# Hybrid decoder step on one core: outer products of the sample states in four row groups of the array, head norms copied to four quadrants

## What is computed

```python
# both head groups: the state is decayed by a number and gets a rank-one update
S = S * exp(g)  + outer(k, beta * (v - exp(g) * S.T @ k))     # delta rule, 128x128
C = C * f       + i * outer(k, v)                             # mLSTM, 128x128
# per head of 128 features, q and k before the recurrence and all outputs after it
q = q * rsqrt(sum(q*q) + eps) * 128**-0.5
k = k * rsqrt(sum(k*k) + eps)
o = o * rsqrt(mean(o*o) + eps) * w * gate
h = concat(o_A, o_B) @ w_out                                  # 264 x 1024 by 1024 x 1024
x = LayerNorm(alpha * x + h)
```

## Time and profile before

| | before |
|---|---|
| median of 3 runs | 1038.25 us (1035.95 to 1038.7) |
| profiled execution, its own time | 1048.3 us |
| its span | 1046.6 us |
| TensorE busy, share of span | 929.4 us, 89% |
| VectorE busy | 408.8 us, 39% |
| ScalarE busy | 175.7 us, 17% |
| GpSimd busy | 226.0 us, 22% |
| mean granted clock of TensorE | 0.931 |

### The profile page before, as it was taken

The page is one execution under the profiler, slowest core; times in us unless marked ns, Lnnn a source line. Parts: engine busy times, 40 slices in busy tenths (PEclk is TensorE's granted clock), DMA queues, the critical chain, the costliest instruction groups (busy, mean ns, idle before and its releaser), DMA issues.

```text
span 1046.6 us, 12023 instructions
## 1 busy us (share of the span) xinstructions
PE 929.4 (89%) x4804; PEld 506.3 (48%) x4804; DVE 408.8 (39%) x829; ACT 175.7 (17%) x309; POOL 226.0 (22%) x334
## 2 busy tenths in 40 slices
PE   6999988998993799999989768989938999999993
PEld 4888867985342333333323366844414333333330
DVE  3799318634546121222224165912272111111115
ACT  0411221223001111111101242211111111110111
POOL 4579962301312511001100200000012111100000
PEclk9999986997996799999999978979977999999997
DMA  9446639002639589999999915561097789999982
GB/s 261 99 167 249 238 128 312 1 11 93 221 116 394 215 309 407 405 404 399 414 398 427 418 46 160 177 268 46 3 404 294 277 364 409 407 402 404 416 358 83
DMA packets 83578, 277.51 MB, mean 265 GB/s; under 512 B 25337, under 2 KB 44231, under 8 KB 60854
## 3 DMA queue, kind: packets, MB, share of 16 engines
q1 hardware_dynamic: 70298, 255.86, 63.8%
q10 hardware_dynamic: 10660, 16.49, 4.9%
q0 software_dynamic: 2560, 4.33, 1.4%
HBM read 261.49 MB, written 18.01 MB: 267 GB/s over the span
## 4 chain that ended last, share of the span: by engine, by line
PE 73%; DMA 16%; DVE 6%; ACT 2%; issue 1%; ACTq 1%; POOL 0%; SPq 0%; DVEq 0%; POOLq 0%
PE ps L1756 17%; DMA ring<-in_moe_w_up 13%; PE ps L320 11%; PE ps L1780 7%; PE ps L2427 6%; PE ps L1798 3%; PE ps L761 3%; PE ps L1735 3%; PE ps L2304 2%; PE ps L736 1%; DMA work<-in_ln_ffn_b 1%; PE ps L609 1%; PE ps L2274 1%; PE ps L1434 1%; PE ps L1486 1%
## 5 line engine op out<-in xcount | busy, mean ns | idle before, releaser
L1756 PE MATMUL ps<-ring,work 128*64 128x512 f32 x480 | 217.3, 604 | 10.0 <-DMA ring<-in_moe_w_up 8.5
L1757 PE MATMUL ps<-ring,work 128*64 128x512 f32 x480 | 217.4, 604 | 0.0
L1756 PEld LDWEIGHTS ps<-ring,work 128*64 128x64 f32 x480 | 63.6, 138 | 136.5 <-issue 120.6
L1840 DVE TENSOR_TENSOR work<-ps,work 64x512 f32<-64x512 f32 x32 | 33.8, 1056 | 221.7 <-ACT work L1811 221.7
L320 PE MATMUL ps<-work,ring 128*128 128x264 f32 x512 | 115.2, 387 | 0.0
L1780 PE MATMUL ps<-ring,work 128*64 128x512 f32 x248 | 113.0, 598 | 2.3 <-DVE work L1845 1.4
L1781 PE MATMUL ps<-ring,work 128*64 128x512 f32 x248 | 113.1, 598 | 0.0
L320 PEld LDWEIGHTS ps<-work,ring 128*128 128x128 f32 x512 | 96.8, 190 | 16.4
L1202 POOL TENSOR_TENSOR ring<-ring 128x512 f32<-128x512 f32 (+5 forms) x76 | 90.5, 1208 | 9.0 <-DVE ring L1198 5.7
L1850 DVE COPY work<-ps 64x512 f32<-64x512 f32 x32 | 22.2, 694 | 150.7 <-PE ps L1781 150.7
L1861 POOL COPY work<-work 64x1 int32<-64x1 int32 x32 | 5.7, 178 | 336.2 <-PE ps L1735 298.2
(11 more groups left out here) (496 smaller groups left out, 1248.3 us busy)
## 6 DMA issues: line engine op xcount, KB each, us to landing
ring<-in_moe_w_down SPq DMA_DIRECT2D x31, 2048.0 KB, 16.0
ring<-in_moe_w_gate SPq DMA_DIRECT2D x60, 1024.0 KB, 14.6
ring<-in_moe_w_up SPq DMA_DIRECT2D x60, 1024.0 KB, 16.8
ring<-in_w_in ACTq DMA_DIRECT2D x6, 2048.0 KB, 8.5
s_out_mats<-ring SPq DMA_DIRECT2D x4, 1280.0 KB, 4.7
ring<-in_w_in SPq DMA_DIRECT2D x2, 2048.0 KB, 10.3
s_in_mats<-ring SPq DMA_DIRECT2D x4, 1024.0 KB, 6.3
ring<-in_w_out SPq DMA_DIRECT2D x1, 4096.0 KB, 17.1
```

Of the source, the lines that this page charges most:

```text
L1756: nc.tensor.matmul(ps[0:SLOT, 5, :], xgT[s][:, c], gate_w[slot][:, c], start=c == 0, stop=c == DC - 1)
L1757: last = nc.tensor.matmul(ps[SLOT:P, 5, :], xgT[s][:, c], up_w[slot][:, c], start=c == 0, stop=c == DC - 1)
L1840: nc.vector.tensor_tensor(hid[s][0:SLOT].rearrange("t (c p) -> t p c", c=4), strided(ps[SLOT:P, 5, :]), strided(sg[s][SLOT:P]), ALU.mult). ...
```

## The change

1. The 0/1 operands that pick a head are now one 64-column row `head_row` with a one in column 31; `head_col(h, n)` is a slice of n columns of it with the one in column h.
2. Both sums of squares are computed four times, once for each quadrant of 32 output partitions (four 32-column matmuls for one 8-column matmul), so that `R` has the 8 head rows in each quadrant. ln and exp run over all 128 partitions. The spreading matmul of head h contracts over the 32 rows of quadrant h % 4.
3. The turning of keys and values to rows is done four times too, by matmuls with the identity instead of one transpose, so `krow` has its 32 rows in each quadrant (`rows_by_quadrant`; the VectorE copies cover 128 partitions).
4. The 16 masked operands become 4: 128 rows by 512, where quadrant r of batch b is the old operand 4b + r (`pair_mask`, eight small VectorE copies at the start, holds the mask).
5. An outer-product batch is four matmuls with 32-row contraction, in the four row groups, into four banks, with one step at the end.
6. The batches stand elsewhere: batch 0 where groups 0 to 2 stood; batch 1 after the spreading matmuls; batches 2 and 3 after k-steps 2 and 6 of tile 0. Batches 2 and 3 use banks 2 and 3 as well, so tile 1 now waits for update 15. VectorE does updates 0 to 3 before the multiplies, 4 to 15 after `merged`.

```diff
-        head_col = view(const, C0["heads"], 8, 8)
+        head_row = view(const, C0["heads"], 64)
+        pair_mask = const[:, C0["cols"] + 8:C0["cols"] + 16].rearrange("p (b c) -> p b c", c=4)
+        def quad(r):
+            return slice(32 * r, 32 * r + 32)
+        def quad_row_of(r, h):
+            return ident[quad(r), 32 * r + h:32 * r + h + 1].to_broadcast([32, P])
+        def head_col(h, n):
+            return head_row[:, 31 - h:31 - h + n]
...
+            for r in range(4):
+                for b in range(2):
+                    nc.vector.tensor_copy(pair_mask[quad(r), b], ident[quad(r), 36 * r + 16 * b:36 * r + 16 * b + 4]).then_inc(*dv.done("pair_mask"))
...
             for h in range(8):
-                last = nc.tensor.matmul(ps[0:8, 0, 0:T], head_col[:, h], sq[:, h], start=h == 0, stop=h == 7)
+                for r in range(4):
+                    last = nc.tensor.matmul(ps[quad(r), 0, 0:T], head_col(h, 32), sq[:, h], start=h == 0, stop=h == 7)
             last.then_inc(*pe.done("ss"))
...
-                nc.tensor.matmul(ps[:, h, 0:T], row_of(h, 8), R[0:8, RA], start=True, stop=True).then_inc(*pe.done(f"rn{h}"))
+                nc.tensor.matmul(ps[:, h, 0:T], quad_row_of(h % 4, h), R[quad(h % 4), RA], start=True, stop=True).then_inc(*pe.done(f"rn{h}"))
...
+        def rows_by_quadrant(dst, columns):
+            for r in range(4):
+                last = nc.tensor.matmul(dst[quad(r)], columns, ident, start=True, stop=True)
+            return last
...
-            nc.tensor.transpose(ps[0:HS, 3, P:2 * P], kq[:, 0], ident).then_inc(*pe.done("krow"))
+            rows_by_quadrant(ps[:, 3, P:2 * P], kq[:, 0]).then_inc(*pe.done("krow"))
...
-        def pe_outer(t, g):
-            t.wait_ge(*po.at(f"vblk{g}"))
-            if g < 3:
+        OUTER_BANK = (4, 5, 6, 7, 4, 5, 6, 7, 2, 3, 4, 5, 6, 7, 2, 3)
+        def pe_outer(t, b):
+            t.wait_ge(*po.at(f"vblk{b}"))
+            if b == 0:
                 t.wait_ge(*dv.at("hB"))
                 t.wait_ge(*ac.at("oA"))
+                t.wait_ge(*dv.at("s_final"))
             else:
-                t.wait_ge(*dv.at(f"new{g - 3}"))
-            nc.tensor.matmul(banks(5 + g % 3), krow[0:HS, 0 if g < 8 else 2], flat(vblk[g % 2][0:HS]), start=True, stop=True).then_inc(*pe.done(f"outer{g}"))
+                t.wait_ge(*dv.at(f"new{(0, 3, 5, 9)[b]}"))
+            if b == 2:
+                t.wait_ge(*dv.at("norm_o7"))
+            for r in range(4):
+                last = nc.tensor.matmul(banks(OUTER_BANK[4 * b + r]), krow[quad(r), 0 if b < 2 else 2], flat(vblk[b % 2][quad(r)]),
+                                        start=True, stop=True)
+            last.then_inc(*pe.done(f"outer{b}"))
...
             for i in range(TT):
+                if i == 1:
+                    t.wait_ge(*dv.at("new15"))
                 residual_pe(t, i, 2 * i)
...
-                    if i == 0 and k < 7:
-                        for g in range(3 + 2 * k, min(5 + 2 * k, 16)):
-                            pe_outer(t, g)
+                    if i == 0 and k in (2, 6):
+                        pe_outer(t, 2 + k // 6)
...
-            nc.scalar.activation(R[0:8, RA], ps[0:8, 0, 0:T], ACT.Ln, bias=eps_rms[0:8], scale=1.0 / DK).then_inc(*ac.done())
+            nc.scalar.activation(R[:, RA], ps[:, 0, 0:T], ACT.Ln, bias=eps_rms, scale=1.0 / DK).then_inc(*ac.done())
...
-            for g in range(16):
+            for b in range(4):
...
+                nc.gpsimd.tensor_tensor(vblk[b % 2], krow[:, 1 if b < 2 else 3].unsqueeze(1).to_broadcast([P, 4, P]),
+                                        pair_mask[:, b % 2].unsqueeze(2).to_broadcast([P, 4, P]), ALU.mult).then_inc(*po.done(f"vblk{b}"))
```

More of the change, by code:

```diff
@@ L582, in mix_pe @@
             t.wait_ge(*dv.at("krow0"))
-            nc.tensor.transpose(ps[0:HS, 3, 2 * P:3 * P], small[:, 3], ident).then_inc(*pe.done("vrow"))
+            rows_by_quadrant(ps[:, 3, 2 * P:3 * P], small[:, 3]).then_inc(*pe.done("vrow"))
             ml_pe_rden(t)
@@ L685, in ml_pe_state @@
                 for i in range(TT):
-                    last = nc.tensor.matmul(ps[0:H, 7, 0:P], head_col[:, h, 0:H], kwk[:, 4 * i + h], start=(h, i) == (0, 0),
+                    last = nc.tensor.matmul(ps[0:H, 7, 0:P], head_col(h, H), kwk[:, 4 * i + h], start=(h, i) == (0, 0),
                                             stop=(h, i) == (H - 1, TT - 1))
@@ L705, in ml_pe_den @@
                 den = ps[0:H, 6, 0:SEQ]
-                nc.tensor.matmul(den, head_col[:, h, 0:H], wexp[:, h, 0:SEQ], start=h == 0, stop=False)
-                last = nc.tensor.matmul(den[:, P:SEQ], head_col[:, h, 0:H], wexp[:, h, SEQ:384], start=False, stop=h == H - 1)
+                nc.tensor.matmul(den, head_col(h, H), wexp[:, h, 0:SEQ], start=h == 0, stop=False)
+                last = nc.tensor.matmul(den[:, P:SEQ], head_col(h, H), wexp[:, h, SEQ:384], start=False, stop=h == H - 1)
             last.then_inc(*pe.done("den"))
@@ L741, in mix_pe_out @@
             for h in range(8):
-                last = nc.tensor.matmul(ps[0:8, 0, 0:T], head_col[:, h], sq[:, h], start=h == 0, stop=h == 7)
+                for r in range(4):
+                    last = nc.tensor.matmul(ps[quad(r), 0, 0:T], head_col(h, 32), sq[:, h], start=h == 0, stop=h == 7)
             last.then_inc(*pe.done("ss_o"))
-            for g in range(3):
-                pe_outer(t, g)
+            pe_outer(t, 0)
             t.wait_ge(*ac.at("rn_o"))
@@ L749, in mix_pe_out @@
                     t.wait_ge(*dv.at(f"norm_o{h - 4}"))
-                nc.tensor.matmul(ps[:, h % 4, 0:T], row_of(h, 8), R[0:8, RA], start=True, stop=True).then_inc(*pe.done(f"rno{h}"))
+                nc.tensor.matmul(ps[:, h % 4, 0:T], quad_row_of(h % 4, h), R[quad(h % 4), RA], start=True, stop=True).then_inc(*pe.done(f"rno{h}"))
+            pe_outer(t, 1)
             t.wait_ge(sem("w_out"), 16)
@@ L928, in mix_dve @@
                 nc.vector.scalar_tensor_tensor(s1[:, h], s1[:, h], cd[:, h:h + 1], bank4(4)[:, h], ALU.mult, ALU.add).then_inc(*dv.done("s_final"))
-            for g in range(3):
+            for g in range(4):
                 dve_new_state(v, g)
@@ L936, in mix_dve @@
             nc.vector.tensor_tensor(oT[:, 4:8], oT[:, 4:8], pj[:, OB:OB + 4], ALU.mult).then_inc(*dv.done("merged"))
-            for g in range(3, 16):
+            for g in range(4, 16):
                 dve_new_state(v, g)
         def dve_new_state(v, g):
-            v.wait_ge(*pe.at(f"outer{g}"))
+            v.wait_ge(*pe.at(f"outer{g // 4}"))
             state, factor = (Sst, EG) if g < 8 else (Cst, FP)
@@ L1019, in mix_pool @@
             nc.gpsimd.tensor_scalar(alpha_id, ident, ALPHA, None, ALU.mult).then_inc(*po.done("alpha_id"))
-            for g in range(16):
-                if g == 0:
-                    pool.wait_ge(*dv.at("krowA"))
-                if g == 8:
-                    pool.wait_ge(*dv.at("rowsB"))
-                if g >= 2:
-                    pool.wait_ge(*pe.at(f"outer{g - 2}"))
-                p = 4 * (g % 8)
-                nc.gpsimd.tensor_tensor(vblk[g % 2][0:HS], krow[0:HS, 1 if g < 8 else 3].unsqueeze(1).to_broadcast([HS, 4, P]),
-                                        ident[0:HS, p:p + 4].unsqueeze(2).to_broadcast([HS, 4, P]),
-                                        ALU.mult).then_inc(*po.done(f"vblk{g}"))
+            for b in range(4):
+                if b == 0:
+                    pool.wait_ge(*dv.at("pair_mask"))
+                if b % 2 == 0:
+                    pool.wait_ge(*dv.at("rowsB" if b else "krowA"))
+                if b >= 2:
+                    pool.wait_ge(*pe.at(f"outer{b - 2}"))
+                nc.gpsimd.tensor_tensor(vblk[b % 2], krow[:, 1 if b < 2 else 3].unsqueeze(1).to_broadcast([P, 4, P]),
+                                        pair_mask[:, b % 2].unsqueeze(2).to_broadcast([P, 4, P]), ALU.mult).then_inc(*po.done(f"vblk{b}"))
         def ab_stores(sp):
```

23 lines of the change are left out of this document (11 added, 12 removed).

## The result

| | before | changed |
|---|---|---|
| median of the runs | 1038.7 us (5 runs, 1035.95 to 1039.51) | 1031.55 us (5 runs, 1030.77 to 1033.31) |
| profiled execution | 1048.3 us, span 1046.6, mean clock 0.931 | 1030.94 us, span 1029.2, mean clock 0.938 |

The ratio is 0.9925 with a 95% interval of 0.9902 to 0.9948: faster, by 7.2 us. Forecast were 1026.6 us (range 1021.5 to 1032.0) and a gain of 11.6. Between the two profiled executions the gain is 17.4 us.

What follows compares the result with a forecast made beforehand. TensorE was taken to bound the mixer, with its gain reaching the end undiminished. Terms of 3.0 - 0.5 + 1.5 + 9.3 - 1.7 = 11.6 us, off 1038.25, gave 1026.6 us, range 1021.5 to 1032.0.

Steps and rivals of the forecast that it cites:

- What bounds the kernel, and that a gain arrives: Mixer: TensorE, busy 89% of the span, holds 73% of the chain; a gain there should reach the end undiminished.
- rival 4: Behind the mixer: the expert weights' start hangs on something else, only some 4 us arrive, 1034 us; chance 0.06.
- The cost of a batch: Outer products: eight passes in four row groups run four at a time, 1.06 us at full clock, 1.9 at half.
- Rival 1: Outer-product batches: row groups overlap only in part, two at a time, costing 4.3 us in all, 1031.0 us; chance 0.13.
- rival 2: Outer-product batches: row groups run one after another, a batch takes 3.6 us, slower at 1043.8 us; chance 0.05.
- First spread: First normalisation: multiplies end 1.9 us earlier and the clock returns earlier, 3.0 us gained in all, bounds 1.9 and 3.4.
- Rows by quadrant: Turning keys and values to rows: four groups of 8 passes for four transposes, 0.5 us lost on TensorE.
- Out of the k-steps and the clock after that stand: Output projection: 9.3 us gained from first k-step to tile 1's end, 1.7 lost at half clock after a 2.5 us wait.
- Rival 3: Tile 1: the clock stays low for the 15.4 us behind the wait, 1040.3 us; chance 0.04.
- rival 5: Mixer: wider tiles keep the clock up, no charge behind the wait, 16.1 us gained, 1022.2 us; chance 0.12.
- Second spread and updates 0 to 3: Second normalisation: the k-steps start at 264.0 instead of 265.56 us, 1.5 us gained; 3.6 at full clock.
- The sum against the median: Whole kernel: the 11.6 us reckoned on the profiled execution was taken off the median, 1038.25 us, giving 1026.6.

## Why the prediction was right in kind and high in size

Point by point, by its own steps.

*What bounds the kernel, and that a gain arrives.* Right. Behind the mixer the changed kernel takes 728.8 and 728.9 us, the kernel before 726.2 to 733.4; no part given back shows in them. The first expert weight is issued 12.8 us earlier, with the mixer's end: rival 4 is out.

*The cost of a batch.* Right: 1.07 us for 1.06. Rival 1 is out by that number; rival 2 is too, and the 3.63 us in one row group are what it would have cost.

*First spread, 3.0 us.* Right: 18.7 or 18.8 us in three profiles before, 15.7 and 15.4 in two after, 3.0 to 3.4 gained. The size came out by luck, as two errors inside it cancel: VectorE's multiplies follow each other in 0.35 us and not in 0.44 (that was the distance at which the eight-row spreads, two passes of 0.22 us, released them), and ended at 151.9 instead of 152.9. With the start of the stage set equal, the multiplies gave 2.6 us and the clock 0.4, where 1.9 and 1.1 were forecast.

*Rows by quadrant, 0.5 us lost.* Possible, not shown. From the decay rows to the second column-sum the kernel before takes 83.5, 84.3 and 83.4 us, the changed one 84.1 and 84.0: at most half a microsecond, no more than the scatter.

*Out of the k-steps and the clock after that stand, 9.3 - 1.7 = 7.6 us.* Right: 43.2 to 43.8 before, 36.2 after, 7.0 to 7.5 gained; the stand 2.43 us, the clock's price 1.8. Rival 3 is out, by the 15.90 us at 1.00 behind the short stretch, and rival 5, by that stretch of 3.3 us at half clock. That the clock fell there at all is not certain in each execution: in the kernel with eight-row spreads it did not.

*Second spread and updates 0 to 3, 1.5 us.* This is the term that failed. Against the execution it was worked out from it is even low: 20.6 less 18.0 is 2.6. But that execution had its clock at 0.50 for 3.3 and 13.0 us in this stage; the other two had 0 and 6.1, and 3.4 and 5.5. Against 16.2 and 17.7 us the changed kernel's 17.9 and 18.0 are no gain but a loss of 0.2 to 1.8. What the batched spread saves there (16 passes in 0.73 and about 2 us), TensorE now stands waiting for VectorE, 2.75 us ahead of spread 4, and batch 1 lies at half clock behind it.

*The sum against the median.* "The median of the runs lies 10 us below it; with the same gain, 1038.25 - 11.6" was the wrong step. It took a gain reckoned in one slow execution for the gain of the median. A mean clock of 0.931 and 10 us above the median were the warning. Of 94 executions of the kernel before in and beside the experiments, with a median of 1039.8 us, not one took as long as 1048.3. The mean time of the 12 with a mean clock under 0.935 is 1044.5, that of the 21 at 0.940 or more 1037.9. A term whose rows lie in a half-clock stretch that the typical execution does not have is not a gain of the typical execution. With the second stage at nothing the sum is 3.0 - 0.5 + 0 + 9.3 - 1.7 = 10.1, 1028.2; the medians, pooled over all series, show 1039.8 - 1031.55 = 8.3. The median of 1031.55 lies above the 1024 to 1029 that had a chance of 0.60, and 0.6 from rival 1's 1031.0. That is chance: rival 1's partial overlap did not occur.

*The remaining 2 us* are not settled. One of them is the second stage, which by the means of the typical profiles is a loss of 1.0 and not nothing: the mixer as a whole gained 9.1. Stage by stage, the second profile of the changed kernel and the third of the kernel before differ by 3.4 in the first stage, -0.6 and -0.2 in the middle, 7.2 in the k-steps, 0.9 behind and 0.2 ahead of the mixer, which makes 10.9 us of span, where the medians differ by 8.3. Five profiles don't show how the second stage and the stretch behind are distributed, and these two alone scatter by 4.4 and 7.2 us in one and the same program.

## What to carry to other kernels

Before costing a change on a profile, ask whether the profiled execution is a typical one: hold its own time and mean clock against the median, and if they differ, find the stretches that ran at half clock and give the terms in them a second value at full clock. Four 32-row matmuls in four row groups cost little more than one, but work taken from an engine opens waits beside it: look where the batch's consumer is then late, and place the batches by when the consumer is done, not evenly. On TensorE, a stand may cost a second time through the clock behind it; filling it with idle matmuls took 5.7 us off the median here, of which the stage with the stands shows 2.4 to 3.0, and moving two batches by a k-step or two took off 2.6.
